# Moving the second gate's modulation products ahead of the output projection, and the second norm's sums early in layer 1

## The reference

```python
c_act = silu(c)
for l in range(2):
    mod = c_act @ mod_w[l] + mod_b[l]
    shift1, scale1, gate1, shift2, scale2, gate2 = split(mod, 6)
    h = rms_norm(x, norm1_g[l]) * (1 + scale1) + shift1
    mix = diff_fox_mixer(h, ...) if l % 2 == 0 else stick_breaking_mixer(h, ...)   # attention @ w_out
    x = x + gate1 * mix
    h = rms_norm(x, norm2_g[l]) * (1 + scale2) + shift2
    x = x + gate2 * hier_moe(h, ...)
```

## Time and profile before

| what | value |
|---|---|
| median of 3 runs | 1301.83 us (1300.61, 1301.83, 1302.54) |
| span of the profiled execution | 1299.5 us |
| PE busy | 924.1 us (71%) |
| DVE busy | 311.2 us (24%) |
| ACT busy | 204.3 us (16%) |
| read from HBM | 488.25 MB, 377 GB/s over the span |
| mean granted TensorE clock | 0.870 |

### The profile page before, as it was taken

How to read it: one execution, slowest core, us unless ns; L and a number is a source line. 1 busy time by engine, 2 the same in 40 slices (tenths; PEclk the granted TensorE clock), 3 DMA queues, 4 the chain that set the end, 5 groups by cost and what they waited for, 6 DMA issues and landing times.

```text
span 1299.5 us, 13607 instructions
## 1 busy us (share of the span) xinstructions
PE 924.1 (71%) x5602; PEld 436.6 (34%) x5602; DVE 311.2 (24%) x614; ACT 204.3 (16%) x423; POOL 32.5 (3%) x95
## 2 busy tenths in 40 slices
PE   6999899566565657475789998976374665655577
PEld 3444455121221213131357665532031212212133
DVE  1548565010010101010147565421010100101011
ACT  2222425010101101000110453420010101010000
POOL 3000000000000000000000121000000000000000
PEclk9999999787887888697999997998786877887789
DMA  9983698999999999999999822699999999999996
GB/s 362 370 284 136 261 423 371 391 428 427 429 428 430 428 430 428 428 427 427 424 404 374 337 71 124 238 405 429 427 428 428 429 430 428 429 428 428 427 424 266
DMA packets 67575, 489.97 MB, mean 377 GB/s; under 512 B 18240, under 2 KB 18368, under 8 KB 37576
## 3 DMA queue, kind: packets, MB, share of 16 engines
q1 hardware_dynamic: 66832, 488.25, 90.7%
q10 hardware_dynamic: 696, 1.07, 0.2%
HBM read 488.25 MB, written 1.05 MB: 377 GB/s over the span
## 4 chain that ended last, share of the span: by engine, by line
DMA 51%; PE 39%; DVE 5%; SPq 2%; issue 1%; ACT 1%; DVEq 0%; ACTq 0%
DMA tokens<-in_moe_w_dram 45%; PE bank L969 11%; PE bank L714 7%; PE bank L1000 5%; PE bank L878 5%; PE bank L764 4%; DMA ring<-in_moe_w_dram 3%; DMA ring<-in_ev_w_in_dram 2%; SPq L439 2%; PE bank L656 1%; PE bank L818 1%; PE bank L834 1%; DVE alone L1525 1%; PE bank L932 1%; PE bank L1009 1%
## 5 line engine op out<-in xcount | busy, mean ns | idle before, releaser
L969 PE MATMUL bank<-ring,region 128*32 128x512 f32 x1472 | 259.5, 667 | 166.4 <-DMA ring<-in_moe_w_dram 80.1
L1000 PE MATMUL bank<-ring,region 128*32 128x512 f32 x832 | 145.7, 729 | 141.0 <-DMA ring<-in_moe_w_dram 87.2
L969 PEld LDWEIGHTS bank<-ring,region 128*32 128x32 f32 x1472 | 69.4, 121 | 341.7 <-issue 276.3
L969 PE MATMUL bank<-work,region 128*32 128x512 f32 x256 | 131.1, 672 | 0.0
L969 PE MATMUL bank<-tokens,region 128*32 128x512 f32 x256 | 131.0, 672 | 0.0
L1000 PEld LDWEIGHTS bank<-ring,region 128*32 128x32 f32 x832 | 38.9, 131 | 234.5 <-issue 199.4
L714 PE MATMUL bank<-ring,tokens 128*128 128x512 f32 x256 | 115.4, 602 | 0.4 <-DMA ring<-in_ev_w_in_dram 0.4
L1851 DVE TENSOR_TENSOR region<-region,bank 128x512 f32<-128x512 f32 x16 | 11.0, 688 | 434.3 <-PE bank L969 434.3
L1858 DVE TENSOR_TENSOR region<-bank,region 128x512 f32<-128x512 f32 x32 | 20.6, 686 | 285.4 <-PE bank L1000 285.4
L1186 ACT ACTIVATE region<-bank,shift,scale 128x128 f32<-128x128 f32 x64 | 24.0, 456 | 381.6 <-PE bank L956 381.6
L956 PE MATMUL bank<-region,h 128*128 128x128 f32 x512 | 63.7, 285 | 10.5 <-issue 9.7
(11 more groups left out here) (253 smaller groups left out, 978.3 us busy)
## 6 DMA issues: line engine op xcount, KB each, us to landing
ring<-in_moe_w_dram SPq DMA_DIRECT2D x144, 2048.0 KB, 19.6
ring<-in_mod_w_dram SPq DMA_DIRECT2D x24, 2048.0 KB, 18.2
work<-in_moe_w_dram SPq DMA_DIRECT2D x22, 2048.0 KB, 24.2
tokens<-in_moe_w_dram SPq DMA_DIRECT2D x22, 2048.0 KB, 28.6
ring<-in_ev_w_in_dram SPq DMA_DIRECT2D x6, 2048.0 KB, 20.3
ring<-in_od_w_in_dram SPq DMA_DIRECT2D x5, 2048.0 KB, 13.2
ring<-in_ev_w_out_dram SPq DMA_DIRECT2D x2, 2048.0 KB, 23.7
alone<-in_moe_w_dram SPq DMA_DIRECT2D x2, 2048.0 KB, 13.1
```

The lines of the kernel that those rows point to most:

```text
L969: last = pe.matmul(bank[which][32 * j:32 * j + 32, :], m.seated[:, k, 32 * j:32 * j + 32], weights(4 * which + j, k * FE), start=(k == 0), ...
L1000: last = pe.matmul(bank[half][32 * j:32 * j + 32, :], m.hidT[:, c, 32 * j:32 * j + 32], w, start=(c == 0), stop=(c == FC - 1), skip_group_ ...
```

## The change

In both layers the two GATE2 units are loaded ahead of the two output units. Their products leave the place behind `attend` and go into its steps: in layer 0 the first unit's at step 14, ahead of `turn_half`, the second's at step 15, ahead of the first `project_out`; in layer 1 both at step 13, one ahead of `turn_half`, one behind it. In layer 0 SECOND's part and columns move from steps 14 and 15 to 12 and 13. In layer 1 SECOND's sums, part and columns move from steps 12, 12 and 14 to 1, 2 and 4 and get bank 5 to themselves; NEXT's sums in layer 0 go to bank 0.

```diff
--- before.py
+++ after.py
@@ -52,7 +52,7 @@
 MOD_UNITS = (4, 2, 4, 2, 4)
 
 
-LAST_DENSE = [("out", 0), ("out", 1), (GATE2, 0), (GATE2, 1)]
+LAST_DENSE = [(GATE2, 0), (GATE2, 1), ("out", 0), ("out", 1)]
 
 
 
@@ -95,9 +95,10 @@
 LATE_LOADS_AT = 11
 ALONE_AT = 1
 APART_AT = (2, 7)
-SECOND_PART_AT = (14, 12)
-SECOND_COLS_AT = (15, 14)
-ADD_SUMS_AT = (17, 12)
+SECOND_PART_AT = (12, 2)
+SECOND_COLS_AT = (13, 4)
+ADD_SUMS_AT = (17, 1)
+GATE2_AT = ({14: (0,), 15: (1,)}, {13: (0, 1)})
 
 
 NEXT_SUMS = {0: 2, 1: 2, 2: 2, 3: 2, 4: 2, 5: 1, 6: 1, 14: 1, 15: 1}
@@ -646,9 +647,11 @@
         slot = full(l, MOD_AT[l][group][e])
         if group == SECOND and e == 0:
             pe.wait_ge(s["proj_copied"], TT * IN_UNITS * (l + 1))
-        if group == GATE2 and e == 0:
-            pe.wait_ge(s["cols_ready"], 3 + l)
-        out, rows = bank[mod_bank(group)], KC // MOD_UNITS[group]
+        if group == GATE2 and e == 0 and l == 0:
+            pe.wait_ge(s["cols_ready"], 2)
+        elif group == GATE2 and e == 0:
+            pe.wait_ge(s["proj_copied"], TT * IN_UNITS * (l + 1))
+        out, rows = bank[mod_bank(l, group)], KC // MOD_UNITS[group]
         w = (slot_rows if rows == 2 else slot_tall)(m, slot)
         for k in range(rows * e, rows * e + rows):
             for i in range(8 // rows):
@@ -667,10 +670,9 @@
     def add_sums(l):
 
         pe.wait_ge(s["cols_summed"], l + 1)
-        pe.wait_ge(s["proj_copied"], TT * IN_UNITS * (l + 1))
         if l == 0:
-            pe.wait_ge(s["cols_ready"], 2)
-        out = bank[mod_bank(SECOND)]
+            pe.wait_ge(s["sc_moved"], NHH)
+        out = bank[0 if l == 0 else mod_bank(l, SECOND)]
         for j in range(4):
             i, half = divmod(j, 2)
             last = pe.matmul(out[32 * j:32 * j + 32, :], m.ones[:, 0:32], m.cols_sum[i][:, half * COL:(half + 1) * COL],
@@ -846,6 +848,8 @@
             pe.wait_ge(s["cum_copied"], 2)
         if half == 1 and lo == 0:
             pe.wait_ge(s["proj_copied"], TT * IN_UNITS * (l + 1))
+            if l == 1:
+                pe.wait_ge(s["cols_ready"], 4)
         pT = m.pT[w % 2]
         o0, o1 = (bank[o_bank(half, t)][:, lo:lo + wide] for t in range(TT))
         v0, v1 = (m.v[:, t, out:out + wide] for t in range(TT))
@@ -909,8 +913,12 @@
                 mod_cols(l, SECOND)
             if l == 0 and 2 <= step < 6:
                 turn_qk(step + 2)
+            for e in GATE2_AT[l].get(step, ())[:1]:
+                mod_products(l, GATE2, e)
             if step == O_TURN_AT[l]:
                 turn_half(l, 0)
+            for e in GATE2_AT[l].get(step, ())[1:]:
+                mod_products(l, GATE2, e)
             if O_OUT_AT[l] <= step < O_OUT_AT[l] + 4:
                 project_out(l, 0, step - O_OUT_AT[l])
         turn_half(l, 1)
@@ -1086,8 +1094,6 @@
             pe.wait_ge(s[done], HT_STEPS * l + 4)
         project_early(l)
         attend(l)
-        for e in range(2):
-            mod_products(l, GATE2, e)
         turn_tokens(2 * l + 1)
         route(l)
         experts(l)
@@ -1113,14 +1119,14 @@
     return 6 + i % 2 if half == 0 or i < 2 else i - 2
 
 
-def mod_bank(group):
-
-    return (0, 2, 3, 3)[group]
+def mod_bank(l, group):
+
+    return (0, 2, 5 if l else 3, 3)[group]
 
 
 def cols_bank(l, group):
 
-    return 1 if l == 0 and group == FIRST else 3
+    return mod_bank(l, group) if group == SECOND else 1 + l
 
 
 def modulation(m, n):
@@ -1466,7 +1472,7 @@
             dve.wait_ge(s["sums_added"], 1 + (group == SECOND))
         else:
             wait_dense(dve, m, l, MOD_AT[l][group][-1])
-        out, b = m.part, bank[3 if l == 1 else mod_bank(group)]
+        out, b = m.part, bank[mod_bank(l, group)]
         if group == FIRST:
             dve.wait_ge(s["cols_made"], 2 * l)
         elif group == SECOND:
@@ -1658,6 +1664,8 @@
             soften(step)
             if step == SECOND_PART_AT[0]:
                 mod_part(0, SECOND)
+            if step == SECOND_COLS_AT[0]:
+                mod_cols(0, SECOND)
             if step >= 2 and step % 2 == 0 and step <= 8:
                 subtract_parts(step // 2 - 1)
             if 1 <= step <= 4:
@@ -1668,7 +1676,6 @@
                 norm_heads()
             sum_next(summed, NEXT_SUMS.get(step, 0))
             summed += NEXT_SUMS.get(step, 0)
-        mod_cols(0, SECOND)
         sum_next(summed, NEXT_LAST)
         dve.sem_inc(s["cols_summed"], 1)
         for i in range(2):
@@ -1723,9 +1730,10 @@
             break_stick(step)
             if step == SECOND_PART_AT[1]:
                 mod_part(1, SECOND)
+            if step == SECOND_COLS_AT[1]:
+                mod_cols(1, SECOND)
             if step == O_READY_AT[1]:
                 copy_out(0)
-        mod_cols(1, SECOND)
         add_first_half(1)
         copy_out(1)
         add_out(1, 0, 3)
```

## The result

The changed kernel takes 1310.99 us (median of 6 runs, 1308.44 to 1317.89) against 1302.18 of the kernel before (6 runs): a ratio of 1.0065, 95% interval 1.0046 to 1.0085, which is +8.5 us (6.0 to 11.1). Forecast were +3.2 us and a range that ended at 1309.5: the direction is right, the size is not. The profiled execution has a span of 1311.0 us against 1299.5, 11.5 more, so its pieces add up to 3 us more than the medians differ by.

The account below looks back on a forecast made before the run. Transfers bound the expert stages and PE the dense stages, so the release of expert units 8 and on sets the end. Layer 0 +8.1 and layer 1 -4.9 give +3.2: 1301.8 to 1305.0 us, range 1300 to 1309.5.

Parts of the forecast that it names:

- Layer 0's wait: First output product waits for its unit's later landing, starting at 174.8 instead of 168.09: +6.7 us; no-wait rival 0.12.
- The clock's share: Layer 0, after PE's new 3.2 us rest: 3.0 us at half clock, +1.5 us (bounds 0 and 6.7).
- Layer 0 in sum: All layer 0 terms, +6.7 + 1.5 - 0.1: +8.1 us.
- Layer 1's heads: Layer 1 up to the output product's end, at full clock: -5.7 us; rival with clock low there 0.15.
- the rest of 1.46 us at step 13: Layer 1, step 13: a new PE wait for ACT's copy, about 1.5 us, as long as one that lowered the clock.
- The norm behind the products: Both ends: ACT's norm becomes late, so moving products gains 0.1 to 0.2 us of 3.57 per layer; full-gain rival 0.05.
- The clock at the end of the dense stage: Low clock after PE's new rests at the ends: nothing in layer 0, 0.9 us in layer 1; clock-spared rival 0.18.
- PE's two new rests: End of each dense stage, where GATE2's products leave: PE rests 2.3 and 1.1 us.
- layer 1 in sum: All layer 1 terms, -5.7 plus 0.9 for the end's clock, less 0.1 gained there: -4.9 us.
- layer 0's row at 213: Layer 0's existing low stretch, 213 to 217; its four us all at half clock gave layer 1's end bound of 2.0.
- the 13.4 us row: Layer 1's long low stretch, 786.90 to 800.30, granted 0.50; half its length gave layer 0's clock bound of 6.7.

Follow-up runs that it names:

- one unit fewer ahead: Kernel before, layer 0 changed with only its first GATE2 unit loaded ahead of the output units and used at step 14, the second last: ratio 1.0017, +2.2 us.
- layer 0 alone: The change made in layer 0 only, layer 1 as in the kernel before: ratio 1.0063, +8.2 us.
- the same with its end filled: The change in layer 0 only, plus five and two dummy matmuls in PE's two rests at layer 0's end: ratio 1.0056, +7.3 us.
- the change with its ends filled: The whole change plus five and two dummy matmuls in PE's two rests at each layer's end: ratio 1.0015, +2.0 us against the kernel before.
- with end and wait filled: The change in layer 0 only, dummy matmuls at its end and seven before the first output product: ratio 1.0033, +4.3 us.
- one unit each, filled: Layer 1 only changed, one GATE2 unit at step 13, one behind the last output product, one and two dummy matmuls in the end's rests: ratio 0.9955, -5.9 us.
- the dummies in the gap: Kernel before with layer 1's SECOND work early, GATE2 loaded and used last, four and four dummy matmuls at layer 1's step 13: ratio 0.9980, -2.6 us.
- with one unit each: Layer 1 only changed, first GATE2 unit at step 13, second behind the last output product, no dummy matmuls: ratio 0.9972, -3.6 us.
- layer 1 alone: The change made in layer 1 only, layer 0 as in the kernel before: ratio 1.0002, +0.3 us.
- the filled kernel: The change in layer 1 only, plus five and two dummy matmuls in PE's two rests at layer 1's end: ratio 0.9965, -4.6 us.
- GATE2 between the halves: Kernel before with layer 0's GATE2 units loaded between the output units and used between the output projection's halves: ratio 1.0051, +6.6 us.

## Why the prediction was wrong, step by step

**Layer 0's wait: right.** Forecast +6.7 from the landing; 6.8 in the trace, 1.7 with one unit fewer ahead. The Trainium skill, "DMA: Bandwidth & Descriptors" (Queues, rings and completion order), has descriptors of a queue consumed in ring order; the landings agree, 26.6 us from issue in the third place and 5.1 us less one place ahead. The wait of 3.2 us was measured at 3.19. The clock's share, +1.5, is 1.7 in three traces (5.40 us for 3.70: layer 0 alone, the same with its end filled, the change with its ends filled) and absent in that of the change itself, where the clock stayed full. In the medians the landing's 6.7 isn't confirmed: with end and wait filled they give 4.3 (3.0 to 5.7).

**Layer 0 in sum: right.** Forecast +8.1, measured +8.2 (6.6 to 9.9) with layer 0 changed alone. The agreement to 0.1 is luck: its trace has 6.8 and 1.7 for the wait and its end 0.9 shorter than in that of the kernel before, where the forecast had -0.1.

**Layer 1's heads: right.** Forecast -5.7 up to the last output product; -5.7 to -5.8 in five traces. In that of the change it is -4.9: the rest of 1.46 us at step 13, which the prediction named, was followed by 3.4 us of low clock. It is -2.6 in that of one unit each, filled, where the clock fell at the end of a later rest of 1.99 us. The trace of the dummies in the gap has the -5.8 with the products left in their old place, so it is the clock and the early columns, and not where the products stand; in the medians that kernel gains only 2.6.

**The norm behind the products: right.** The first tile is turned 2.35 us after the last output product, the second at 4.49; moving products away from there gained 0.3 us at most (28.6 us for layer 1's end with one unit each, 28.9 before, neither with low clock).

**The clock at the end of the dense stage: the step that failed.** The prediction said of PE's two new rests: in layer 0 "I charge nothing; in layer 1 there is none, and I charge 0.9 (bounds 0 and 2.0)". Layer 1's end lengthened by 4.1 us, in the change and with layer 1 alone, and filling it gave 4.8 back. By the medians layer 1 in sum was +0.3 and not -4.9, and these 5.2 us are the whole miss (8.5 for 3.2). The clock's 4.8 for the 0.9 charged make 3.9 of them; the rest is that the filled kernel gained 4.6 and not 5.8, and its trace has 0.9 of that in a low stretch still left in its end. In layer 0, where nothing was charged, filling the end gave 0.9 us, within the noise. The error was to take the length of one low stretch from layer 0's row at 213 as the bound. What came was two: 3.4 us, under the second tile's turning and the gate's row, and after some 3 us at full clock another of 6.8, under the second gate row and the placing of x, 512 columns wide matmuls that go half as fast and on which the routing waits. The bounds for the clock were asked for from both sides, and the 13.4 us row of the same group should have been the upper one here as it was for layer 0's wait; with its 6.7 for the 0.9 the sum would have reached 1310.8.

**What stays open.** Why the second stretch comes. It does so in layer 0 with the cover in place too: the ends of 31.7 in four kernels whose layer 0 is as before have 6.8 us of it, that of the kernel before 3.4. In layer 1 it is over 6 us long in both traces with the cover gone and nothing filled, 3.4 us in the four where dummies stand in the gap or at the end, absent with one unit each, and of the six with layer 1 unchanged one has 3.4. It begins during or just behind the router's products, 36 columns wide, in all; whether they are the cause was not tried. Layer 0's two uncovered ends in which it did not come (29.3 and 29.0) show that one trace can't price it; the medians do.

## What to carry to other kernels

Work that looks late may be cover: before moving it, follow the other engines' chain that ends in the same place, and price both the wait and the clock under what comes behind it; a handful of dummy matmuls in the rest tells the two apart, and may be all that is wanted. In a saturated queue a load moved ahead of another delays that one by its full length (5.1 us for 2 MB), so an order of loads has to be checked against the first use of each load that it pushes back. A price taken from one low stretch is no bound; take the longest in the trace.

## What the runs showed of the hardware

PE can be busy for all of 5.9 us and still be at 1.2 GHz, and fall to it without a rest, behind matmuls of 36 columns (213 to 217 in the earlier trace rows, with PE busy throughout). The Trainium skill, "TensorE: Matmul & The Clock Gate" (What's actually happening), ties the low clock to idleness; this case has it with none just before, and the measurement decides. Rests of 1.5 and of 3.2 us were followed by low clock in some traces and not in others whose programs are the same up to there: the wait of 3.19 us cost nothing in the trace of the change and 1.7 us with layer 0 alone, and the rest of 1.46 us at step 13 was followed by low clock in the change and not with layer 1 alone. Low clock under a stretch in which PE would rest later anyway can cost nothing (109.20 us with 3.4 us of it, with one unit each in layer 1, as without). The spread of a kernel's runs doesn't sort by whether the rests are filled: it is 9.5 us for the change and 11.6 for GATE2 between the halves, but 3.6 for layer 0 alone, unfilled (6 runs), and 8.1 for the change with its ends filled (12 runs).
